# A gated delta-rule kernel: z in channel-major layout, the turning of T before the sixth level on the vector engine, and levels one to five on the changing columns only

## What is computed

```
for every token t (one value head, key and value width 128 in GDN, 64 in RWKV)
    state = decay_t * state + (update built from k_t, v_t and state)
    y_t   = state applied to q_t (r_t in RWKV)
GDN:  y = rmsnorm(y) * norm_w * silu(z),   z = h @ w_z
```

## Time and profile before

| | |
|---|---|
| median of 3 runs | 1746.42 us (1746.22 to 1752.28) |
| profiled execution | 1754.11 us, span 1752.3 us, mean granted clock 0.982 |
| PE busy | 1615.6 us, 92% of the span |
| DVE, ACT, POOL busy | 882.4, 659.2, 122.4 us |
| DMA | 210.95 MB |

### The profile page before, as it was taken

One profiled execution on the slowest core, in us unless ns is written; L12 is line 12 of the kernel. 1 busy time (PEld: TensorE's weight loads), 2 busy tenths in 40 slices (PEclk: granted clock), 3 DMA queues, 4 the chain that ended last, 5 costly groups with the idle time before them and its releaser, 6 DMA issues.

```text
span 1752.3 us, 36626 instructions
## 1 busy us (share of the span) xinstructions
PE 1615.6 (92%) x15044; PEld 1017.5 (58%) x15044; DVE 882.4 (50%) x1880; ACT 659.2 (38%) x1316; POOL 122.4 (7%) x311
## 2 busy tenths in 40 slices
PE   6999999999899999999999999999999888777798
PEld 2465565655645667777767676767744544333343
DVE  1372541725423758686868686868610641111163
ACT  2151531515312655555555555555500111111113
POOL 7000010000000000000000000000000022111100
PEclk9999999999999999999999999999999989899999
DMA  9230110301202211111111111111054579999731
GB/s 362 86 99 2 48 49 2 95 0 49 97 19 75 76 50 49 50 49 50 49 50 49 50 49 50 49 50 49 2 204 172 215 292 419 421 421 401 313 154 48
DMA packets 105462, 210.95 MB, mean 120 GB/s; under 512 B 10194, under 2 KB 78135, under 8 KB 92028
## 3 DMA queue, kind: packets, MB, share of 16 engines
q1 hardware_dynamic: 99256, 197.52, 31.1%
q0 software_dynamic: 4896, 8.40, 1.3%
q10 hardware_dynamic: 1188, 3.28, 0.5%
HBM read 203.80 MB, written 14.81 MB: 125 GB/s over the span
## 4 chain that ended last, share of the span: by engine, by line
PE 53%; DMA 10%; DVE 4%; ACT 2%; issue 2%; SPq 0%; DVEq 0%; ACTq 0%; POOL 0%; POOLq 0%
PE ps L1462 12%; DMA W<-in_moe_w_up_dram 7%; PE ps L2501 5%; PE ps L1473 5%; PE ps L1634 4%; PE ps L1603 4%; PE ps L3083 3%; PE ps L2897 3%; DMA W<-in_moe_w_gate_dram 3%; PE ps L506 2%; PE ps L1503 2%; PE ps L1484 1%; PE ps L1513 1%; PE ps L1525 1%; PE ps L1488 1%
## 5 line engine op out<-in xcount | busy, mean ns | idle before, releaser
L1462 PE MATMUL ps<-hT,W 128*128 128x512 f32 x512 | 231.8, 597 | 2.2 <-ACTq L95 2.2
L1462 PEld LDWEIGHTS ps<-hT,W 128*128 128x128 f32 x512 | 95.6, 192 | 99.8 <-issue 98.0
L594 PE MATMUL ps<-hT,W 128*128 128x512 f32 x288 | 138.4, 610 | 4.3 <-DVE spare L189 4.3
L1473 PE MATMUL ps<-W,hT 128*128 128x256 f32 x512 | 126.1, 393 | 0.0
L2045 DVE SCALAR_TENSOR_TENSOR arena<-ps,arena 128x510 f32<-128x510 f32 (+1 forms) x128 | 95.4, 746 | 14.0 <-ACT arena L1764 10.6
L1473 PEld LDWEIGHTS ps<-W,hT 128*128 128x128 f32 x512 | 94.6, 193 | 13.4
L2501 PE MATMUL ps<-W,yT 128*128 128x512 f32 x216 | 93.1, 592 | 0.9 <-ACT yT L1857 0.9
L1867 ACT ACTIVATE W<-ps 128x512 f32<-128x512 f32 x96 | 57.5, 599 | 70.8 <-PE ps L1603 30.7
L594 PEld LDWEIGHTS ps<-hT,W 128*128 128x128 f32 x288 | 50.3, 189 | 51.7 <-issue 49.9
L1634 PE MATMUL ps<-W 64*64 64x64 f32 x2304 | 77.1, 220 | 0.0
L2974 ACT ACTIVATE arena<-arena 128x256 f32<-128x256 f32 x48 | 20.0, 417 | 148.8 <-DVE arena L2611 137.9
(11 more groups left out here) (535 smaller groups left out, 2881.0 us busy)
## 6 DMA issues: line engine op xcount, KB each, us to landing
W<-in_w_in_dram SPq DMA_DIRECT2D x33, 512.0 KB, 6.5
W<-in_gdn_w_in_dram SPq DMA_DIRECT2D x16, 1024.0 KB, 7.5
arena<-in_moe_w_up_dram SPq DMA_DIRECT2D x16, 1024.0 KB, 5.9
arena<-in_moe_w_down_dram SPq DMA_DIRECT2D x16, 1024.0 KB, 9.9
W<-in_moe_w_up_dram SPq DMA_DIRECT2D x16, 1024.0 KB, 5.9
W<-in_moe_w_down_dram SPq DMA_DIRECT2D x16, 1024.0 KB, 5.8
W<-in_moe_w_gate_dram SPq DMA_DIRECT2D x16, 1024.0 KB, 6.0
arena<-in_moe_w_gate_dram SPq DMA_DIRECT2D x14, 1024.0 KB
```

The lines of the kernel that those rows point to most:

```text
L594: mm = pe.matmul(ps[:, 5 + i % 2, :], w[:, k, j, :], hT[:, k, :], start=(k == 0), stop=(k == ND - 1))
L1462: mm = pe.matmul(ps[:, 6 + k0 % 2, :], wg[:, k, j * P:(j + 1) * P], hT[:, k, :], start=(k == 0), stop=(k == ND - 1))
L1473: mm = pe.matmul(ps[:, 4 if t < 2 else 1, 256 * (t % 2):256 * (t % 2) + 256], hT[:, k, t * P:(t + 1) * P], wz[:, k, :], start=(k == 0), st ...
```

## The change

**z.** The roles of the two operands are exchanged: 128 channels of `wz` are the weights and all 512 tokens of `hT` move. A head has 16 matmuls of 512 columns instead of 32 of 256. z then has channels in the partitions, like `yT`. The norm's weight becomes one value per partition and goes into `silu_z`. The gate is applied after the transposition of o, by DVE, from PSUM straight into `yT` (`gated_y`, two of 128x512 per head); `z_weighted`, the gate over 128x1024 and ACT's `keep_y` are gone, and `z_clamped` follows `gated_y`.

**Level 6.** The flips and ACT's copies of them are gone. After the put of level 5 DVE transposes the missing 32x32 blocks, two instructions per group in GDN and one per head in RWKV, and T V of level 6 waits for them.

**Levels 1 to 5.** Only the columns that change move through PE, are copied by ACT and are put by DVE: 32 columns per tile instead of 64. At level 5 the matmuls had 32 columns already; there ACT's and DVE's widths are halved. The start of the inverse is made by four puts of 64x128 per group instead of two of 64x512. Tiles are numbered so that those with their upper half changing come first (`tile_of`, `MIXED`), and POOL makes the masks in the narrower form.

```
+def changing(ap, lv, second):
+    return ap.rearrange("p (k s x) -> p k s x", s=2, x=1 << lv)[:, :, second, :]
...
-            def flipped(h, name):
-                q = HALF[0]
-                for c in range(NT):
-                    mm = pe.matmul(ps[q, (2, 7)[h], c * HD:(c + 1) * HD], TTc[q, h, c, :], ident[q, q], start=True, stop=True)
-                mm.then_inc(*rw_pe.step(name))
...
-                                mm = pe.matmul(ps[q, 1 + 3 * h, c * HD:(c + 1) * HD], N_[q, h, c, q], TTc[q, h, c, :], start=True, stop=True)
+                                mm = pe.matmul(ps[q, 1 + 3 * h, c * QB:(c + 1) * QB], N_[q, h, c, q], changing(TTc[q, h, c, :], lv, 1), start=True, stop=True)
                     mm.then_inc(*rw_pe.step(f"V {h} {lv}"))
-                    if top:
-                        flipped(h, f"T {h} {lv}")
...
-                    pe.wait_ge(*rw_act.at(f"T {h} {lv}" if top else f"V {h} {lv}", n))
-                    if not top:
-                        pe.wait_ge(*rw_dve.at(f"turned {h} {lv}", n))
+                    pe.wait_ge(*rw_act.at(f"V {h} {lv}", n))
+                    pe.wait_ge(*rw_dve.at(f"turned {h} {lv}", n))
...
+                            for q in HALF:
+                                mm = pe.matmul(ps[q, 3 + 3 * h, c * QB:(c + 1) * QB], Tc[q, h, c, :], Vch[q, h, c, :], start=True, stop=True)
...
-                    if lv == LEVELS - 1:
-                        act.wait_ge(*rw_pe.at(f"T {h} {lv}", n))
-                        act.activation(Tc[q, h, :, :].rearrange("p c t -> p (c t)"), ps[q, (2, 7)[h], 0:NT * HD], ACT.Copy)\
...
+                        dve.copy_predicated(changing(TTc[:, h, :, :].rearrange("p c t -> p (c t)"), lv, 1),
+                                            quad[:, lv, 0, :, :].rearrange("p c t -> p (c t)").rearrange("p (n x) -> p n x", x=1 << lv),
+                                            ps[:, 3 + 3 * h, 0:NT * QB].rearrange("p (n x) -> p n x", x=1 << lv))\
...
+                if lv == LEVELS - 2:
+                    for h in range(2):
+                        dve.wait_ge(*rw_dve.at(f"T {h} {lv}", n))
+                        dve.transpose(Tc[QUARTER[1], h, :, 0:QB], TTc[QUARTER[0], h, :, QB:HD]).then_inc(*rw_dve.step(f"turned {h} {lv + 1}"))
...
+    def narrow(bank, m):
+        return ps[:, bank, m * QB:(m + 1) * QB]
...
+    MIXED = (0, 4, 1, 5, 2, 6, 3, 7)
...
+        def z_part(s, e, ks=range(ND)):
+            if e == 0 and ks[0] == 0:
                 pe.wait_ge(*(gz_in.at("in", s.ago.i) if s.ago else (gz0_in, 16)))
                 pe.wait_ge(*s.dve.at("norm eps 0", s.i))
                 pe.wait_ge(*s.dve.at("norm eps 1", s.i))
             for k in ks:
-                mm = pe.matmul(ps[:, 4 if t < 2 else 1, 256 * (t % 2):256 * (t % 2) + 256], hT[:, k, t * P:(t + 1) * P],
-                               wz[:, k, :], start=(k == 0), stop=(k == ND - 1))
-            if t % 2 and ks[-1] == ND - 1:
-                mm.then_inc(*s.pe.step("z half" if t == 1 else "z"))
+                mm = pe.matmul(ps[:, (4, 1)[e], :], wz[:, k, e * P:(e + 1) * P], hT[:, k, :], start=(k == 0), stop=(k == ND - 1))
+            if ks[-1] == ND - 1:
+                mm.then_inc(*s.pe.step("z" if e else "z half"))
...
-                            for m in (0, 2, 1, 3, 4, 6, 5, 7):
-                                to, of = HALF if m % 4 < 2 else HALF[::-1]
-                                mm = pe.matmul(small(3 * g, m)[to, :], Nn[of, 2 * g + m // 4, m % 4, to], TTgc[of, g, m, :], start=True, stop=True)
+                            for m in MIXED:
+                                to, of = HALF if m < 4 else HALF[::-1]
+                                mm = pe.matmul(small(3 * g, m)[to, :], Nn[of, g, m, to], TTgc[of, g, m, :], start=True, stop=True)
                         elif joined:
-                            for m in (0, 2, 1, 3, 4, 6, 5, 7):
+                            for m in MIXED:
                                 for to, _, of, cols in across(m):
-                                    mm = pe.matmul(small(3 * g, m)[to, cols], Nn[of, 2 * g + m // 4, m % 4, to], TTgc[of, g, m, cols], start=True, stop=True)
+                                    mm = pe.matmul(narrow(3 * g, m)[to, :], Nn[of, g, m, to], TTgc[of, g, m, cols], start=True, stop=True)
                         else:
                             for m in range(8):
                                 for q in HALF:
-                                    mm = pe.matmul(small(3 * g, m)[q, :], Nn[q, 2 * g + m // 4, m % 4, q], TTgc[q, g, m, :], start=True, stop=True)
+                                    mm = pe.matmul(narrow(3 * g, m)[q, :], Nn[q, g, m, q], changing(TTgc[q, g, m, :], lv, m < 4), start=True, stop=True)
                         mm.then_inc(*s.pe.step(f"V {g} {lv}"))
-                        if top:
-                            pe.wait_ge(*s.act.at(("k tokens", "v tokens")[g], s.i))
-                            pe.nop().then_inc(admitted, 1)
-                            for m in (0, 2, 1, 3, 4, 6, 5, 7):
-                                q = HALF[m % 4 // 2]
-                                mm = pe.matmul(small((4, 7)[g], m)[q, :], TTgc[q, g, m, :], ident[q, q], start=True, stop=True)
-                            mm.then_inc(*s.pe.step(f"Tt {g} {lv}"))
                     if st == 0 and lv == 1:
-                        z_part(s, 2, range(3))
+                        z_part(s, 1, range(1))
                     if st == 0 and joined:
-                        z_part(s, 3, range(2))
+                        z_part(s, 1, range(4, 5))
                     if st == 1 and top:
-                        z_part(s, 3, range(4, ND))
+                        z_part(s, 1, range(6, ND))
                     if st:
                         g = st - 1
                         if g == 1 and joined:
-                            z_part(s, 3, range(2, 4))
-                        pe.wait_ge(*s.act.at(f"T {g} {lv}" if top else f"V {g} {lv}", s.i))
+                            z_part(s, 1, range(5, 6))
+                        pe.wait_ge(*s.act.at(f"V {g} {lv}", s.i))
                         if scan and lv == 1 and g == 0:
                             pe.wait_ge(*s.act.at(f"qS {NT - 1}", s.i))
-                        if not top:
...
-            z_part(s, 0)
+            z_part(s, 0, range(0, 4))
             attended(s, 3)
-            z_part(s, 1)
+            z_part(s, 0, range(4, ND))
...
-        def keep_y(s, e, ago):
-            if ago and s.i == 0:
-                return s.act.skip(f"ago y {e}")
-            kind = "ago " if ago else ""
-            act.wait_ge(*s.pe.at(f"{kind}o^T {e}", s.i))
-            k = 2 * ((LOOPS if s.i is None else s.i) - (1 if ago else 0)) + e
-            act.activation(yT[:, k, :], ps[:, 3 + e, :], ACT.Copy).then_inc(*s.act.step(f"{kind}y {e}"))
...
+                    width = 8 * HD if lv == LEVELS - 1 else 8 * QB
+                    act.activation(Vgc[:, g, :, :].rearrange("p m t -> p (m t)")[:, 0:width], ps[:, 3 * g, 0:width], ACT.Copy).then_inc(*s.act.step(f"V {g} {lv}"))
...
+            dve.scalar_tensor_tensor(out=zg, in0=zg, scalar=nw[:, 0:1], in1=zr, op0=ALU.mult, op1=ALU.mult).then_inc(*s.dve.step("silu z"))
...
-        def o_gated(s):
-            dve.wait_ge(*s.dve.at("o normed", s.i))
-            dve.wait_ge(*s.dve.at("z weighted", s.i))
-            dve.tensor_tensor(flat8, flat8, zg.rearrange("p c (e t) -> p (c e) t", e=2), ALU.mult).then_inc(*s.dve.step("gated"))
+        def gated_y(s, ago):
+            kind = "ago " if ago else ""
+            for e in range(2):
+                if ago and s.i == 0:
+                    s.dve.skip(f"ago y {e}")
+                    continue
+                of = s.ago if ago else s
+                dve.wait_ge(*of.dve.at("silu z", of.i))
+                dve.wait_ge(*s.pe.at(f"{kind}o^T {e}", s.i))
+                k = 2 * ((LOOPS if s.i is None else s.i) - (1 if ago else 0)) + e
+                dve.tensor_tensor(yT[:, k, :], ps[:, 3 + e, :], zg[:, e, :], ALU.mult).then_inc(*s.dve.step(f"{kind}y {e}"))
...
+        def changed(g, lv):
+            x = 1 << lv
+            tiles = TTgc[:, g, :, :].rearrange("p m t -> p (m t)")
+            return bass.AP(tensor=tiles.tensor, offset=tiles.offset + x, ap=[tiles.ap[0], [4 * HD - x, 2], [2 * x, 4 * QB // x], [1, x]])
         def put_blocks(s, g, lv):
             hold(dve).then_inc(*s.dve.step())
-            dve.copy_predicated(TTgc[:, g, :, :].rearrange("p (c b) t -> p c b t", c=2), masked(lv), tiles4(ps[:, 3 * g + 2, :]))\
-               .then_inc(*s.dve.step(f"T {g} {lv}"))
+            dve.copy_predicated(changed(g, lv), quad[:, lv, :, :, :].rearrange("p d n t -> p d (n t)").rearrange("p d (n x) -> p d n x", x=1 << lv),
+                                ps[:, 3 * g + 2, 0:8 * QB].rearrange("p (d n x) -> p d n x", d=2, x=1 << lv)).then_inc(*s.dve.step(f"T {g} {lv}"))
             if lv < LEVELS - 2:
                 dve.wait_ge(*s.dve.at(f"T {g} {lv}", s.i))
```

(46 more changed lines are left out.)

93 lines of the change are left out of this document (40 added, 53 removed).

## The result

The changed kernel takes 1736.99 us in the median of 20 runs (1728.39 to 1757.91), the kernel before 1750.40 us of 20 (1745.65 to 1754.94). The ratio is 0.9929, 95% interval 0.9911 to 0.9947: 12.4 us faster, where 21 were forecast; the ratio leaves out the changed kernel's slowest execution, which is over 1.5% above its fastest. The kernel before stays within 9.3 us, the changed one spreads over 29.5: its runs at a mean granted clock of 0.981 to 0.984 take 1728 to 1735 us, those at 0.968 to 0.970 take 1746 us and more. So there are two results: what the change saves at an undisturbed clock, and how much of that the clock takes back. The profiled execution took 1737.7 us with a clock of 0.975.

The account below looks back on a forecast made before the run. PE, busy 92% of the span, was taken as the bound. GDN heads -12.6 us (-1.57 by 8), RWKV -6.4 and last head -2.0 made -21.0, from 1746.42 to 1725.5 us; range 1707 to 1741.

Parts of the forecast that it names:

- clock term: GDN levels: clock falls in four of eight heads instead of two, 2.0 us each, +0.5 us per head.
- third rival: Levels 1 to 4 of each head: halved columns make the clock fall, 2.0 us per fall, about 1770 us; 8%.
- Flips: Level 6: 32 fewer PE records at 30.3 ns, -0.97 us per GDN head; RWKV -1.0 us per pair.
- Code wait: GDN level 5: 96 fewer instructions to fetch shorten the unnamed 1.34 us wait by about 0.9 us per head.
- Narrow columns: GDN levels 1 to 4: weights set the matmul time, so halving moving columns gains 0 on PE.
- first rival: GDN levels: narrower matmuls pay on PE, 3.3 us per head, half of it kept: -13, so 1712 us; 15%.
- Start of level 1: GDN: narrower puts of the start save 0.3 of PE's 0.6 us wait per head.
- RWKV's puts and copies: RWKV levels: shorter put and copy save 0.6 us per pair, bounds 0 and -0.85.
- Last head: After the last GDN head: gate and `z_weighted` leave the chain, -2.35, with +0.35 back: -2.0 us.
- z: GDN z matmuls, 16 of 512 columns for 32 of 256: no gain on PE, 64 fewer instructions per head.

Follow-up runs that it names:

- rw_wide: Changed kernel with PE streaming and ACT copying all 64 columns in RWKV levels 1 to 4: 1730.38 us, ratio 0.9881.
- rw_wide_again: Second measurement of rw_wide, the same kernel: 1731.97 us, ratio 0.9885.
- gdn_new: Changed kernel with rw_wide's edit and RWKV's flips back on PE with ACT's copies: 1730.31 us, ratio 0.9881.
- wide_zsplit: Changed kernel with rw_wide's edit and one z matmul moved between the two V of GDN's level 6: 1735.33 us, ratio 0.9923.
- wide_first: Changed kernel with rw_wide's edit and 64 columns in levels 1 to 4 of the first GDN head only: 1730.00 us, ratio 0.9878.
- rw_new: Kernel before with only RWKV's part of the change, GDN as before: 1748.41 us, ratio 1.0007.
- after: The changed kernel itself, first measurement against the kernel before: 1736.99 us, ratio 0.9929; its profiled execution took 1737.7 us.
- after_again: The changed kernel measured once more, without an edit: 1737.16 us, ratio 0.9941; its profiled execution took 1737.88 us.
- gdn_pad: Changed kernel with 96 empty PE instructions per GDN head in the source, of which the executed program has no trace: one run, 1751.92 us.

## Why the prediction was wrong

The direction and the time lay where they were said to, but the gain is six tenths of the forecast.

The step that failed is the clock's. The prediction put falls in the GDN levels alone, at 0.5 us per head, 4 us together, and its third rival, too, placed them in "levels 1 to 4 of each head". The mechanism, narrower columns and then a lower clock, was the right one, and the place and the price were wrong. The levels of RWKV were narrowed as well, and the sum had no clock term for them. There a fall cost not 2.0 but 12 us, because the clock stayed low for 27.3 us, over full-width projections too; in each of the two heads of before that gave the 2.0 it was low for 3.4 us. In the GDN heads behind the first loop head, where the term was placed, neither profile of the changed kernel has a fall. So the clock took 11.6 us (24 less 12.4) where 4 were forecast.

How much of the 11.6 us is RWKV's is known less well. The 32 executions of the changed kernel have a median of 1737.1 us, the 27 with 64 columns in RWKV and narrow GDN heads 1731.3 (rw_wide, rw_wide_again, gdn_new, wide_zsplit, and wide_first with its one wide head): 5.7 us less, although wide columns cost 1.6 in the pairs. That makes about 7 us. In rw_new 4 us of gain at full clock came out as 1.2 of loss, so 5. By the ratios of rw_wide and gdn_new alone it would be 12; wide_zsplit shows hardly any of it. The direction is shown both ways, the size lies around 5 to 7. The rest are falls in the last pair, which every profile has, and in the first GDN heads; I haven't taken them apart. rw_wide changes PE's columns and ACT's copies together, and no run separates the two.

Without the clock the sum was 25 us and the runs show 24, but by terms that erred both ways.

- Flips: -0.97 was 32 records at the mean price of the mixed stretch. They weren't on the path in full: the net is -0.53. V alone takes 1.41 us, 0.34 of it the step to group 1, which waits for the last put of level 5; a step of 0.27 us stood at this place before too. In RWKV V alone takes 67.0 ns a record and mixed with flips 46, so the flips ran half beside V, on the other rows; the prediction had read the earlier trace rows, one kind alone, as the price of both.
- Code wait: the mechanism was right and is now shown. In the profiles of after and after_again it went altogether, level 5 lost 1.39 us instead of 0.9. It isn't gone for good: gdn_pad, rw_wide, rw_wide_again and wide_first, whose GDN heads but the first are the same, have a wait without a name of 0.6 to 1.2 us in one or two heads.
- Narrow columns: 0.55 to 0.61 us per head, not 0 and not the first rival's 3.3. The near rows were the better guide.
- Start of level 1: 0 instead of -0.3. The wait for the puts was followed so closely by one for ACT's copy of z that only its name changed.
- RWKV's puts and copies: -0.57, forecast -0.6. rw_wide's 108.58 against 108.19 says that 0.4 of it hangs on PE's and ACT's columns.
- Last head: 0 instead of -2.0. The gate left DVE's chain, and `gated_y` of the head before came into it, of much the same length (its row is below). PE had the 40 records of the output projection (line 2402, now 2398) to execute before the end in either case. Of the 42 us before the end PE was idle for 2.7 before and for 3.0 after.

```profile
1240.32 1.29 DVE yT L2151 x2
```

- z: 0, as said.

## What to carry to other kernels

Fewer moving columns in matmuls of small tiles saved almost nothing here (0.55 of 16 us in GDN), and in RWKV they let PE's clock fall while PE was busy. The price of a fall is how long the clock stays low, 27.3 us here, over whatever stands behind the narrowed stretch, not what that stretch itself loses. Compare the spread and the mean clock of twenty executions, not a median of three, before and after such a change. When operations of two kinds are interleaved in the trace, the mean per record isn't what removing one of them gives: time one kind alone.

## What was not expected of the hardware

A fall's length differs from one execution to the next at the same place of the same kernel: in the levels of the last RWKV pair the low clock lasted 10.2 us in after and 23.9 in after_again, 20.5 in rw_wide and 17.1 in rw_wide_again; in the kernel before it was 6.8. And a wait for code repeats at the same instruction of every head only while a head is a whole number of transfers long, as it was with 8; the changed head has 7 in one and 8 in the next, and in its two profiles none of the undisturbed heads waits.
